# Routing tile by tile between half projections, and four of six shared-expert products inside the experts' loop

## The reference, cut to what matters

```python
h = layer_norm(ALPHA * x + merged @ w_out, ln1_g, ln1_b)
scores = sigmoid(h @ w_router)                      # 128 experts
_, idx = top_k(scores + b_router, 8)
sel = take_along_axis(scores, idx)
gate = sel / sum(sel) * 2.5
# each routed expert, on the tokens that chose it, times their gate:
yb = (silu(xb @ w_e1[e]) * (xb @ w_e3[e])) @ w_e2[e] * w
shared = (silu(h @ w_s1) * (h @ w_s3)) @ w_s2       # hidden width 256
y = layer_norm(ALPHA * h + shared + routed, ln2_g, ln2_b)
```

## Time and profile before

| what | us |
|---|---|
| median of 3 runs | 2056.1 (2052.11 to 2059.55) |
| profiled execution | 2052.74, its span 2051.0 |
| block of `stage_mix_experts` begins | 777.2 in the span |
| loop's first matmul | 913.7 |
| loop's last scatter | 1977.2 |
| PE busy over the span | 1804.3 (88%) |
| DVE, ACT, POOL busy | 628.6, 385.2, 362.8 |
| mean DMA rate over the span | 259 GB/s |

### The profile page before, as it was taken

One profiled execution on the slowest core, in us unless ns is written; L12 is line 12 of the kernel. 1 busy time (PEld: TensorE's weight loads), 2 busy tenths in 40 slices (PEclk: granted clock), 3 DMA queues, 4 the chain that ended last, 5 costly groups with the idle time before them and its releaser, 6 DMA issues. The chain is left out here.

```text
span 2051.0 us, 28955 instructions
## 1 busy us (share of the span) xinstructions
PE 1804.3 (88%) x10578; PEld 1052.1 (51%) x10578; DVE 628.6 (31%) x1490; ACT 385.2 (19%) x915; POOL 362.8 (18%) x529
## 2 busy tenths in 40 slices
PE   7999996888999997999888887988888888888887
PEld 6857766887778883473333333433333333333332
DVE  1387745774214312242111111111111111111127
ACT  0115543442120101111111111111111111111102
POOL 1000002888850000001111111111010101110100
PEclk9999998999999999999999899999898989998998
DMA  3443312011243325139999999999999999999976
GB/s 116 143 137 102 104 31 47 3 34 35 67 148 97 87 57 206 75 140 420 420 421 413 416 412 412 408 418 408 404 409 398 410 398 406 408 413 400 407 295 253
DMA packets 160782, 532.04 MB, mean 259 GB/s; under 512 B 22061, under 2 KB 88927, under 8 KB 110205
## 3 DMA queue, kind: packets, MB, share of 16 engines
q1 hardware_dynamic: 138971, 488.63, 60.6%
q0 software_dynamic: 20640, 41.23, 5.4%
q10 hardware_dynamic: 1098, 1.18, 0.2%
HBM read 522.52 MB, written 41.42 MB: 275 GB/s over the span
## 5 line engine op out<-in xcount | busy, mean ns | idle before, releaser
L1942 PE MATMUL bank<-arena 128*64 128x512 f32 x2048 | 517.8, 664 | 152.0 <-DMA arena<-in_w_e 150.3
L1942 PEld LDWEIGHTS bank<-arena 128*64 128x64 f32 x2048 | 160.1, 152 | 508.5 <-issue 507.0
L1960 PE MATMUL bank<-arena 128*64 128x512 f32 x1024 | 233.8, 598 | 0.0
L2134 DVE TENSOR_TENSOR arena<-bank,arena 128x256 f32<-128x256 f32 x64 | 27.2, 425 | 601.2 <-ACT arena L2006 601.2
L1824 POOL DMA_INDIRECT arena<-h_rows,index x66 | 66.9, 1013 | 775.7 <-DVE index L2025 728.5
L1422 PE MATMUL bank<-arena 128*128 128x276 f32 x768 | 184.7, 399 | 7.3 <-ACT arena L1524 3.1
L1422 PEld LDWEIGHTS bank<-arena 128*128 128x128 f32 x768 | 146.4, 191 | 41.7 <-ACT arena L1524 3.5
L1201 PE MATMUL bank<-arena 64*64 64x64 f32 (+2 forms) x2816 | 126.3, 245 | 27.5 <-DVE arena L1314 14.7
L2006 ACT ACTIVATE arena<-bank 128x256 f32<-128x256 f32 x64 | 24.7, 386 | 621.0 <-PE bank L1942 621.0
L1201 PEld LDWEIGHTS bank<-arena 64*64 64x64 f32 x2816 | 111.0, 140 | 34.3 <-DVE arena L1314 15.8
L1960 PEld LDWEIGHTS bank<-arena 128*64 128x64 f32 x1024 | 67.8, 136 | 110.9 <-issue 109.7
(11 more groups left out here) (323 smaller groups left out, 1840.0 us busy)
## 6 DMA issues: line engine op xcount, KB each, us to landing
arena<-in_w_e SPq DMA_DIRECT2D x384, 1024.0 KB, 14.8
arena<-in_w_in SPq DMA_DIRECT2D x50, 512.0 KB, 4.2
arena<-routed_rows SPq DMA_DIRECT2D x8, 2048.0 KB, 23.2
arena<-in_w_mem_kv SPq DMA_DIRECT2D x4, 1024.0 KB, 5.9
arena<-in_cache_mem_k SPq DMA_DIRECT2D x8, 512.0 KB, 4.6
arena<-in_cache_mem_v SPq DMA_DIRECT2D x8, 512.0 KB, 5.4
arena<-in_w_out SPq DMA_DIRECT2D x2, 2048.0 KB, 11.3
arena<-in_w_s SPq DMA_DIRECT2D x3, 1024.0 KB, 10.5
```

Of the source, the lines that this page charges most:

```text
L1942: mm = pe.matmul(p_gu[t * S:(t + 1) * S, :], xt[:, v, c, t * S:(t + 1) * S], w13[2 * v + t][:, :, c, :], start=(c == 0), stop=(c == KD - 1))
L1960: mm = pe.matmul(p_y[h][t * S:(t + 1) * S, :], hidT[:, j, t * S:(t + 1) * S], w2[2 * v + t][:, j, h * 512:(h + 1) * 512], start=(j == 0), ...
```

## The change

The head is reordered, and part of the shared expert moves:

- The router's weights and bias are loaded at the end of the merge, behind `rwkv_ready` (new L1416, L1417). PE waits for them only ahead of product(2).
- PE's products 2 to 4 are cut in halves of four k-steps: first half, route(i-2), second half, turn_h(i-1). The tile of 40 rows has its two halves of columns in the upper and lower rows of banks (`z_bank`). Routing uses banks 6 and 7 in turn.
- ACT writes sigmoids straight from the bank, tile by tile. The norm is two fused instructions rather than three.
- DVE runs `pick(i)` (top eight, and a running sum `counts`) and `weigh(i)` (rank, gate, info) for each tile: tiles 0 and 1 behind norm(2) and norm(3), tile 2 ahead of norm(4), tiles 3 and 4 behind it.
- Queue places come from 6 products: `upper` times picked plus `ones` times counts.
- The shared expert's first layer is six groups (two halves j by three thirds of 184 tokens). Two are made in the head, in halves between the slot products; four in the loop, behind the outputs of pairs 0, 2, 4 and 7, under `If`. ACT and DVE close each of these under `If` too. `ssil` shrinks to two thirds, `yg`, `hid` and `sil` move.
- POOL's two filling loads of `xg` read `x_prompt` rather than `h_rows` and start earlier.

The diff, cut:

```diff
@@ merge, sync
+        sp.wait_ge(sem("rwkv_ready"), 1)
+        sp.dma_start(m.at(O_WR, KD, NE), io["w_router"][0].rearrange("(k p) n -> p k n", p=P)).then_inc(sem("router_loaded"), 16)
+        sp.dma_start(m.at(O_BR, NE), io["b_router"][0:1, :].to_broadcast([P, NE])).then_inc(sem("router_bias_loaded"), 16)
@@ offsets
-SHARED_BANKS = ((7, 3), (1, 2), (7, 3), (1, 2))
-SHARED_GROUPS = ((0, 0), (1, 0), (0, 1), (1, 1))
+THIRD = NT // 3
+EARLY_GROUPS = ((0, 0, 3), (0, 1, 7))
@@ experts, gpsimd
             pool.wait_ge(s_mean, NTT)
+            pool.wait_ge(sem("h_rows_out_0"), 32)
+            for v in range(2):
+                pool.dma_start(xg[:, v, :], io["x_prompt"][0, 0:P, :]).then_inc(s_out[v], 16)
+            for v in range(2):
+                pool.wait_ge(s_out[v], 16)
             pool.wait_ge(sem("h_rows_out_0"), 48)
             pool.wait_ge(sem("h_rows_out_1"), 32)
-            for v in range(2):
-                pool.dma_start(xg[:, v, :], io["h_rows"][0:P, :]).then_inc(s_out[v], 16)
@@ experts, tensor
+            def shared_half(x, j, first, bank):
+                for k in range(KD):
+                    mm = pe.matmul(m.ps[bank][:, x * THIRD:(x + 1) * THIRD], ws[x][:, k, j * P:(j + 1) * P],
+                                   m.arena[:, ds(first + O_HT + k * NT, THIRD)], start=(k == 0), stop=(k == KD - 1))
+                return mm
+            def shared_late(j, first, done):
+                pe.wait_ge(s_sa, done)
+                shared_half(0, j, first, 7)
+                shared_half(1, j, first, 7).then_inc(s_sh, 1)
...
+            product(0, range(KD))
+            product(1, range(KD))
+            turn_h(0)
             pe.wait_ge(sem("router_loaded"), 16)
-            product(0)
-            for i in range(NTT):
-                if i + 1 < NTT:
-                    product(i + 1)
...
+            for i in range(2, NTT):
+                product(i, first)
+                route(i - 2)
+                product(i, second)
+                turn_h(i - 1)
+            route(NTT - 2)
+            turn_h(NTT - 1)
+            route(NTT - 1)
...
-            shared(2)
-            for n in range(AHEAD):
-                find_slots(n, n, n)
-            shared(3)
+            shared(0, 0)
+            find_slots(0, 0, 0)
+            shared(1, 0)
+            find_slots(1, 1, 1)
+            pe.wait_ge(s_rc, NTT - 1)
+            shared(0, 1)
             count = rounds(pe)
-            pe.wait_ge(s_sa, 4)
             pe.wait_ge(s_in[0], 16)
             turn(0)
+            shared(1, 1)
+            pe.wait_ge(s_sa, 1)
...
                         mm.then_inc(s_y, 1)
+                        if v == 0:
+                            with pe.If((NP // 2) * r + i < 3):
+                                shared_late(1, i * THIRD, i + 2)
+                        else:
+                            with pe.If((NP // 2) * r + i < 4):
+                                with pe.If(i > 2):
+                                    shared_late(0, 2 * THIRD, 5)
@@ experts, scalar: for tile 4
+                if i == NTT - 1:
+                    scores(i - 2)
+                square(i)
...
+                else:
+                    root(i)
+                    copy_h(i - 1)
+            scores(NTT - 2)
+            copy_h(NTT - 1)
+            scores(NTT - 1)
...
+                        if u == 0:
+                            with act.If((NP // 4) * r + i < 2):
+                                act.wait_ge(s_sh, 2 * i + 3)
+                                act.activation(ssil[:, 0, :], m.ps[7][:, 0:THIRD], ACT.Silu).then_inc(s_ss, 1)
@@ experts, vector: new helpers, called for each tile
+            def pick(i):
+                dve.wait_ge(s_rc, i + 1)
+                dve.tensor_tensor(sel, score[:, i, :], bias, ALU.add)
+                dve.drain()
+                dve.max(top8[:, i, :], sel)
+                dve.drain()
+                dve.match_replace(rest[:, i, :], top8[:, i, :], sel, -1e30)
+                dve.drain()
+                if i < NTT - 1:
+                    dve.tensor_tensor(picked[:, i, :], rest[:, i, :], sel, ALU.not_equal)
+                    dve.drain()
+                    dve.tensor_tensor(counts[:, i + 1, :], counts[:, i, :], picked[:, i, :], ALU.add).then_inc(s_pick, 1)
...
+            def weigh(i):
+                dve.scalar_tensor_tensor(out=gated, in0=picked[:, i, :], scalar=1.0, in1=score[:, i, :],
+                                         op0=ALU.mult, op1=ALU.mult, accum_out=den[:, i:i + 1])
+                dve.tensor_tensor_scan(rank, m.ones[:, :], picked[:, i, :], 0.0, ALU.mult, ALU.add)
+                dve.tensor_scalar(rest[:, i, :], picked[:, i, :], -ABSENT, ABSENT, ALU.mult, ALU.add)
...
+                        if u == 0:
+                            with dve.If((NP // 4) * r + i < 2):
+                                dve.wait_ge(s_ss, 2 * i + 3)
+                                dve.tensor_tensor(m.arena[:, ds(2 * THIRD * i + O_SACT + NT, THIRD)], m.ps[7][:, THIRD:2 * THIRD], ssil[:, 0, :],
+                                                  ALU.mult).then_inc(s_sa, 1)
```

More of the change, by code:

```diff
@@ L1692 @@
 assert O_XTE + 2 * KD * P <= O_WS[0]
-O_YG = O_HT
+O_YG = O_SSIL + 2 * THIRD
 O_HE = O_YG + 2 * D
@@ new lines, in _ @@
+            dve.memset(counts[:, 0, :], 0.0)
+            dve.tensor_scalar(rows8, m.row[:, :], float(TOPK), -1.0 - FAR, ALU.mult, ALU.add)
+            for i in range(NTT):
+                dve.tensor_scalar(info[:, i, 0:NE, 0], m.ones[:, :], m.row[:, i:i + 1], -FAR, ALU.mult, ALU.add)
+            dve.wait_ge(sem("score_zeroed"), 1)
+            dve.wait_ge(sem("ln1_loaded"), 32)
+            dve.wait_ge(sem("router_bias_loaded"), 16)
+            norm(0)
+            norm(1)
+            for i in range(2, NTT):
+                if i == NTT - 1:
+                    pick(i - 2)
+                    weigh(i - 2)
+                norm(i)
+                if i < NTT - 1:
+                    pick(i - 2)
+                    weigh(i - 2)
@@ L2095, in _ @@
-            for i in range(NTT):
-                dve.tensor_scalar(info[:, i, 0:NE, 0], m.ones[:, :], m.row[:, i:i + 1], -FAR, ALU.mult, ALU.add)
-                dve.tensor_scalar(info[:, i, 0:NE, 1], rank[:, i, :], rows8[:, i:i + 1], None, ALU.add)
-                dve.tensor_scalar(info[:, i, 0:NE, 2], gated[:, i, :], scale[:, i:i + 1], None, ALU.mult)
-            dve.tensor_scalar(rest, picked, -ABSENT, ABSENT, ALU.mult, ALU.add)
-            dve.drain()
-            dve.tensor_copy(info[:, :, NE:NEP, :], info[:, :, 0:NEP - NE, :])
```

233 lines of the change are left out of this document (119 added, 114 removed).

## The result

| | us, median (runs) | ratio to before, 95% interval |
|---|---|---|
| before | 2054.88 (2052.11 to 2059.55, 4) | |
| changed | 2026.85 (2023.02 to 2027.39, 4) | 0.9857 [0.9838, 0.9875] |
| forecast | 2034.7, range 2027 to 2044 | |

The changed kernel is 28.0 us faster by the medians, 1.4%. Of the profiled executions before's took 2052.74 and the changed kernel's 2027.02, 25.7 less.

The account below looks back on a forecast made before the run. The loop was taken as bound by its weight transfers, so time cut from the head comes off the end. Head gains of 23.4 less 2.0 in the loop give 21.4: 2056.1 - 21.4 = 2034.7 us, range 2027 to 2044.

Parts of the forecast that it names:

- Step 1, the router's weights: At the block's start: weights already on the chip, so PE's wait for them goes; gain 4.25 us.
- Step 2, the products: First matmul to last product's end: routes stand between product halves, a tile takes 17.0 instead of 17.8; gain 2.6 us.
- Step 3, last product to last route: Head, behind the last product: chain of tile 4's norm now bare, 14.3 us instead of 14.9; gain 0.6.
- The slow matmuls behind the idle time: At route(3), last transpose and part of route(4): PE at 1.2 GHz after idling 4.8 us; 2.5 us more (1.5 to 4.5).
- The table load: ACT, ahead of the norm's root: 1.28 us by the trace; the skill page's extra drain of some 1.38 left out.
- Step 4, to the first one-hot: Last route to first one-hot: only tile 4's sigmoid, pick, weigh and place left, 5.2 us instead of 17.3; gain 12.1.
- Step 5, to the loop: First one-hot to the loop: slots, transpose and three half groups, 12.6 us instead of 16.5; gain 3.9.
- the margin of one us: Ahead of the loop: gathered rows land at 885.4, one us before PE's transpose at 886.4.
- The loop: Late group behind pair 0 takes 5.3 us against a cover of 3.3, one hole in the stream; cost 2.0, between 0 and 6.
- The branches: The `If`s in all 64 pairs of the loop: taken at nothing, under a room of 3.7 us a pair.
- The rival "no slow level": Head and loop: PE keeps its fast clock and the cover holds, 2.5 + 2.0 us more gained, 2030; chance 0.13.

Follow-up runs that it names:

- a_router_late: The changed kernel with the router's weights loaded at the block's start again, PE waiting for them ahead of product(0): 2025.66 us, ratio 0.9876.
- a_two_full_banks: The changed kernel with both column halves of the 40-row tile again in rows 0 to 39 of their banks: 2027.13 us, ratio 0.9898.
- a_norm_first: The changed kernel with the norm of tile 4 ahead of pick and weigh of tile 2 on DVE: 2019.46 us, ratio 0.9854.
- a_no_late: The changed kernel without the four late shared groups and all conditional branches, so part of the computation is missing: 2019.61 us, ratio 0.9852.
- b_side_by_side: The kernel before with only the 40-row tile's column halves placed in rows 0 to 39 and 64 to 103: 2047.37 us, ratio 0.9979.

## Why the prediction had the mechanism and missed the size

The mechanism stood: a bound stream of 64 pairs, whose start sets the end. The time lies outside the range, by less than the scatter of the runs, but the miss behind it is no chance: the head is shorter than forecast by 5.8 us.

- **Step 1, the router's weights.** Forecast 4.25, measured 4.35 in the place and 3.85 at the loop by `a_router_late`. Right.
- **Step 2, the products.** This is the term that failed: forecast a gain of 2.6, measured 10.5. I priced tile 4 at 15.95 with a product of 13.9 like any other. The product took 7.3. `z_bank` puts the two column halves of a 40-row tile in rows 0 to 39 and 64 to 103, and so they run in half the time of two that follow each other; side by side is the reading of that. The rows of before showed such a pair, there of two experts: 32 matmuls of L1942 with a stationary of 64 columns, written to rows 0 to 63 and 64 to 127, take 7.09, 32 of L1853 with 128 columns 13.90. I used both and compared neither. `a_two_full_banks` gives the price: 6.9 at the product, 3.6 at the loop. Its product, with tile 4 at full length, still ends at 79.9 and not at the forecast 81.0; this other 1.1 of the step is that a full tile took 16.4 (825.31 to 841.71) instead of 17.0. The Trainium skill has the rule in "TensorEngine Tiling (Array Packing)", section "Overview": a small dimension of 64 or less lets two parts of the array work at once, up to twice as fast. The runs agree, 7.07 against 13.9.
- **Step 3, last product to last route.** Forecast a gain of 0.6, measured a loss of 2.2 (14.9 to 17.1), because VectorE came 4.5 us late. Step 2 named "each norm, pick and weigh together is under 9 us of a tile's 17" as the cover, but tile 4's own time fell to 9.2 (842.67 to 851.85), and two picks and weighs stand ahead of its norm: from the norm of tile 3 (841.91) to that of tile 4 (856.36) VectorE needs 14.5 us. The price itself was low too, a norm, pick and weigh with their waits for ScalarE take 9.6 and 10.9 for tiles 2 and 3; at 17 us a tile that would have done no harm. With the product at full length the step measures 14.4 against 14.3, and its idle time 4.56 against 4.8. So this error is the shadow of step 2, and `a_norm_first` gives it back, 3.6. The slow matmuls behind the idle time: 1.7 at route(3) (3.78 against 2.05), within the 1.5 to 4.5 that I had. In `a_two_full_banks` they come to 3.6 (route(3), turn and route(4) against 2.05, 0.70 and 1.96), 1.1 over the 2.5 of the sum, and the rest of the step is 1.0 under its terms, so that 14.4 against 14.3 is in part luck.
- **The table load.** As in the row of before, the root starts at once, 0.02 us behind a load of 1.28 (859.50 and 860.80), and ScalarE was at work up to 0.01 us ahead of the load. The drain of 1.38 us that the Trainium skill counts on top, in "ScalarE: Activation LUTs", section "What ACT_TABLE_LOAD costs", isn't there. The sum rightly had none of it.
- **Step 4, to the first one-hot.** Forecast 5.2, measured 5.6 (868.97 to 874.53). Right but for 0.5: tile 3's weigh ended 0.9 behind the start of tile 4's sigmoid (869.92 and 869.00) and held up its pick. In `a_two_full_banks` it didn't, and the step took 4.9.
- **Step 5, to the loop.** Forecast 12.6 (its terms add up to 12.7), measured 11.7: slots, transpose and handing over were each priced a little high. The gather started at 878.18, landed at 881.56, and PE turned its rows at 882.75, without a wait, so the margin of one us held.
- **The loop.** Forecast one hole of 2.0 us behind pair 0 and nothing later; measured 1.5 in the windows, and between 0.9 and 2 in the loads, by what one compares with. Right, and PE's first waits for weights are 1.4 us at the eighth pair and 2.6 at the tenth (the forecast had the eighth to tenth).
- **The branches.** Nothing, as taken. The Trainium skill's rule in "Runtime: NRT & Kernel Launch", section "Instruction fetch mechanics", has a taken branch hold the engine for a transfer when its target lies outside the two pages in hand; whether these short jumps ever leave them, no run here shows. `a_no_late`, which has none of them, isn't faster by anything that the loads show.

Together: 3.6 of the 5.8 are shown by undoing `z_bank`. The other 2.2 are the distance that `a_two_full_banks` still keeps to the forecast, 110.9 against 113.1: 1.1 in the products, 0.2 in step 4 and 0.9 in step 5, read from the traces and not tested alone. The measured head less the hole is 29.2 - 1.5 = 27.7, close to the 28.0 of the medians. Before's own median lay 1.2 lower with a fourth run than the 2056.1 that the forecast started from; without that the time would lie inside the range. The rival "no slow level" (2030) came nearer by number, but not by what it said, since the slow level was there. The range was too narrow at the fast end: every case in it that was better than forecast was one of waits and clock, none of a changed operation being faster in itself.

## What to carry to other kernels

When a diff changes where an operation writes, price the operation anew, and look in the trace for one of the same shape that is already placed so: the pair 7.09 and 13.90 stood there. When one step gets shorter, check every cover that rested on its old length, on the engine that was to hide under it: half of what PE gained (3.4 of 7.0 us) went to VectorE's queue, and one reordering got 3.6 back. Work that must be done by an engine with slack is cheapest behind the stream, but not before the stream has a full pair in hand: one pair later the same 5.3 us left no hole in the windows.

## What the runs showed of the hardware

- Float32 matmuls of 512 columns with a stationary of 40 columns take half as long in two row ranges of PSUM (rows 0 and 64) as in one: 32 in 7.07 against 13.9 us.
- PE's fall to its 1.2 GHz level came behind idle times of 2.87 to 9.14 us, but also, in `b_side_by_side`, behind two us of six-column products with 0.65 idle in them, and cost 3.0 us there (10.72 against 7.69). The kernel before has the same products and the same 0.65 and kept its clock, so the idle time right ahead doesn't tell alone. The slow stretch falls on what stands behind the idle time: route(3), or the turn and route(4), or all three.
- The start of the stage, behind 770 us of work that is all but the same in these kernels, moved over 7.6 us from one profiled execution to the next.
